# Expert biases in a mixture-of-experts layer: two rows read to one partition each and spread by GpSimd, in place of a 1 MB read to all partitions

## The reference, cut to what matters

```python
gu = lax.ragged_dot(xs, w_gu, group_sizes) + b_gu[sorted_e]     # 1024 -> 2048, the bias is one row of 2048 per expert
gate, up = jnp.split(gu, 2, axis=-1)
gate = jnp.minimum(gate, SWIGLU_LIMIT)
up = jnp.clip(up, -SWIGLU_LIMIT, SWIGLU_LIMIT)
act = (up + 1.0) * (gate * jax.nn.sigmoid(SWIGLU_ALPHA * gate))
out = lax.ragged_dot(act.astype(h.dtype), w_down, group_sizes) + b_down[sorted_e]
out = out * weights.reshape(-1)[order][:, None]
y = jnp.zeros((T, D), dtype=out.dtype).at[tok].add(out)
```

## Time and profile before

| what | value |
|---|---|
| median of the runs | 4029.9 us (4029.44 to 4031.53) |
| the profiled execution's own time | 4033.05 us |
| its span in the profile | 4031.1 us |
| PE busy | 3812.1 us, 95% |
| DVE busy | 2492.9 us, 62% |
| ACT busy | 1613.7 us, 40% |
| POOL busy | 667.9 us, 17% |
| DMA | 813.37 MB, mean 202 GB/s; SP's queue 654.51 MB |
| granted TensorE clock, mean | 0.977 |

### The profile page before, as it was taken

The page is one execution under the profiler, slowest core; times in us unless marked ns, Lnnn a source line. Parts: engine busy times, 40 slices in busy tenths (PEclk is TensorE's granted clock), DMA queues, the critical chain, the costliest instruction groups (busy, mean ns, idle before and its releaser), DMA issues. The chain is left out here.

```text
span 4031.1 us, 66918 instructions
## 1 busy us (share of the span) xinstructions
PE 3812.1 (95%) x17977; PEld 3129.0 (78%) x17978; DVE 2492.9 (62%) x3898; ACT 1613.7 (40%) x2354; POOL 667.9 (17%) x731
## 2 busy tenths in 40 slices
PE   7999999898987999999999999999999999999993
PEld 4887788787876878878877877878888788888782
DVE  5253343596775686576577678577656656656753
ACT  3222321573222464354355455354334434333532
POOL 1110110111221221121111212121121112111202
PEclk9999999899998999999999999999999999999996
DMA  6432441664344797587588787598576667666835
GB/s 236 168 133 84 150 143 69 222 232 150 133 146 154 217 342 221 173 276 225 153 280 286 238 273 257 169 307 266 172 211 208 211 192 230 191 195 180 267 119 190
DMA packets 372676, 813.37 MB, mean 202 GB/s; under 512 B 31449, under 2 KB 31634, under 8 KB 367458
## 3 DMA queue, kind: packets, MB, share of 16 engines
q1 hardware_dynamic: 315826, 654.51, 47.5%
q0 software_dynamic: 53584, 147.48, 14.8%
q10 hardware_dynamic: 3200, 10.53, 0.6%
HBM read 706.18 MB, written 106.23 MB: 202 GB/s over the span
## 5 line engine op out<-in xcount | busy, mean ns | idle before, releaser
L1917 ACT CAST weights_split<-weights_raw 128x1024 fp32r<-128x1024 f32 x468 | 477.7, 1054 | 406.8 <-PE tok_bank_acc L121 284.6
L2012 DVE TENSOR_TENSOR weights_split<-weights_raw,weights_split 128x1024 fp32r<-128x1024 f32 x468 | 545.3, 1217 | 32.4 <-issue 16.4
L2012 DVE TENSOR_TENSOR weights_first<-weights_raw,weights_first 128x1024 fp32r<-128x1024 f32 x464 | 539.1, 1217 | 33.2 <-ACT weights_first L1917 30.3
L1917 ACT CAST weights_first<-weights_raw 128x1024 fp32r<-128x1024 f32 x464 | 471.0, 1050 | 199.3 <-PE tok_bank_acc L121 78.0
L1895 POOL DMA_INDIRECT y_rows<-tok_act_row,tok_token x111 | 200.5, 1806 | 1947.0 <-DVE tok_act_row L2127 1903.6
L119 PE MATMUL tok_bank_acc<-weights_first,weights_split 128*128 128x512 f32 x1136 | 454.3, 400 | 13.4 <-DVE weights_first L2012 10.2
L119 PE MATMUL tok_bank_acc<-weights_split 128*128 128x512 f32 x1136 | 445.4, 392 | 1.2 <-issue 1.1
L121 PE MATMUL tok_bank_acc<-weights_first,weights_split 128*128 128x512 f32 x1136 | 444.1, 391 | 0.0
L120 PE MATMUL tok_bank_acc<-weights_first,weights_split 128*128 128x512 f32 x1136 | 443.1, 390 | 0.0
L121 PE MATMUL tok_bank_acc<-weights_split 128*128 128x512 f32 x1136 | 442.6, 390 | 0.0
L120 PE MATMUL tok_bank_acc<-weights_split 128*128 128x512 f32 x1136 | 442.3, 389 | 0.0
(11 more groups left out here) (377 smaller groups left out, 6838.1 us busy)
## 6 DMA issues: line engine op xcount, KB each, us to landing
weights_raw<-in_w_gu SPq DMA_DIRECT2D x624, 512.0 KB
weights_raw<-in_w_down SPq DMA_DIRECT2D x312, 512.0 KB
tok_bias<-in_b_gu SPq DMA_DIRECT2D x39, 1024.0 KB
early_w_raw<-in_w_in POOLq DMA_DIRECT2D x14, 2048.0 KB, 10.8
proj<-pro_stage SPq DMA_DIRECT2D x112, 256.0 KB, 2.0
pro_w_ada<-in_w_ada POOLq DMA_DIRECT2D x64, 256.0 KB, 3.4
mix_late<-proj SPq DMA_DIRECT2D x48, 256.0 KB, 3.6
mod_w_ada<-in_w_ada SPq DMA_DIRECT2D x8, 1024.0 KB, 15.0
```

Of the source, the lines that this page charges most:

```text
L1917: nc.scalar.copy(whi[c % 2][:, j * SK:(j + 1) * SK], raw[:, n % RAW]).then_inc(hi_done, 1)
L2012: nc.vector.tensor_tensor(wlo[c % 2][:, rows], raw[:, n % RAW], whi[c % 2][:, rows], ALU.subtract).then_inc(lo_done, 1)
```

## The change

The read of 1 MB goes. SP reads the two halves of the next expert's bias row, 1024 floats (4 KB) each, into one partition each, 64 and 96. These lie in the upper half of the tile that now holds both half tile temporaries in its partitions 0 to 63. SP issues them in the middle of a group, after the load of piece 23 and before the loads of the next group's pieces, behind a wait for `bias_set`. POOL spreads each row over the 128 partitions with a `partition_broadcast` into `bias`: for the first group before its loop, and for group g+1 within its turn of group g, after the copies of tokens and shares and before the adds of the down product. It waits there for the group's last activation (which is the last reader of `bias`), for the share copies, the gathered rows and the two bias rows. DVE's first `gate_bias` waits for `bias_set` in place of `bias_in`. The wait for `act_done` on SP goes too.

```diff
-    half_lo, half_gu = k.sb("half_lo", [HR, N]), k.sb("half_gate_up", [HR, N])
+    half_tiles_own = k.sb("half_lo_gate_up", [P, 2, N])
+    half_lo, half_gu = half_tiles_own[0:HR, 0], half_tiles_own[0:HR, 1]
+    bias_rows = [half_tiles_own[p:p + 1].rearrange("p a n -> p (a n)") for p in (HR, HR + 32)]
...
     def sync(sp):
...
         count = field(sp, 0, COUNT, NG)
+        def load_bias_rows(of):
+            for j in range(2):
+                sp.dma_start(bias_rows[j], gu_b[bass.ds(of, 1), j * D:(j + 1) * D]).then_inc(bias_in, 16)
+        load_bias_rows(field(sp, 0, EXPERT, E - 1))
         with sp.Fori(0, NG) as g:
...
-                sp.wait_ge(act_done, G.before * 2 + 1)
-                sp.dma_start(bias[:], gu_b[bass.ds(expert, 1), :].rearrange("o n -> (o n)").partition_broadcast(P)
-                             ).then_inc(bias_in, 16)
                 for n in range(RAW, PIECES * NCH):
                     load(n, expert)
                 next_expert = field(sp, g + 1, EXPERT, E - 1)
                 with sp.If(G.nT > 0):
+                    sp.wait_ge(bias_set, g * 2 + 2)
+                    sp.sem_inc(wait_carrier, 1)
+                    load_bias_rows(next_expert)
                     for n in range(PIECES * NCH, PIECES * NCH + RAW):
                         load(n, next_expert)
...
     def gpsimd(pool):
...
+        def spread_bias(turn):
+            pool.wait_ge(bias_in, turn * 32 + 32)
+            pool.sem_inc(wait_carrier, 1)
+            for j in range(2):
+                nc.gpsimd.partition_broadcast(bias[:, j * D:(j + 1) * D], bias_rows[j], P).then_inc(bias_set, 1)
+                pool.wait_ge(bias_set, turn * 2 + j + 1)
+                pool.sem_inc(wait_carrier, 1)
+        first_full = full_tiles(load_word(pool, 0))
+        pool.wait_ge(rows_in, first_full * 16)
+        pool.sem_inc(wait_carrier, 1)
+        spread_bias(0)
         with pool.Fori(0, NG) as g:
...
                 pool.wait_ge(token_set, g * 2 + 2)
                 pool.sem_inc(wait_carrier, 1)
+                with pool.If(G.nT > 0):
+                    pool.wait_ge(act_done, (G.before + G.U) * 2 + 1)
+                    pool.sem_inc(wait_carrier, 1)
+                    pool.wait_ge(share_set, g * 2 + 2)
+                    pool.sem_inc(wait_carrier, 1)
+                    pool.wait_ge(rows_in, (G.before + G.U + G.nU) * 16)
+                    pool.sem_inc(wait_carrier, 1)
+                    spread_bias(g + 1)
                 for c in (NGU, NGU + 1):
...
         def gate_bias(G, g, q, t):
...
             if q == 0 and t == 0:
-                dve.wait_ge(bias_in, (g + 1) * 16)
+                dve.wait_ge(bias_set, g * 2 + 2)
```

More of the change, by code:

```diff
@@ L1714, in expert_programs @@
      ta_done, ahi_done, alo_done, tx_done, xhi_done, xlo_done, rows_in, y_out0, y_out1, clip_step, wait_carrier,
-     sg_set, word_step, next_set, token_set, share_set, rest_in, pad_set, half_step) = k.sems(
+     sg_set, word_step, next_set, token_set, share_set, rest_in, pad_set, half_step, bias_set) = k.sems(
          "word_set rec_in g2_in g2_set bias_in hi_done lo_done mm_done read_done sg_done act_done "
          "ta_done ahi_done alo_done tx_done xhi_done xlo_done rows_in y_out0 y_out1 clip_step wait_carrier "
-         "sg_set word_step next_set token_set share_set rest_in pad_set half_step")
+         "sg_set word_step next_set token_set share_set rest_in pad_set half_step bias_set")
     rows_left, LEFT = keep["rows_left"], 5
@@ L1728, in weighted_at @@
         if t == HALF:
-            return half_gu[:] if c == NGU + 1 else act_row[0:HR, HALF]
+            return half_gu if c == NGU + 1 else act_row[0:HR, HALF]
         return gu[:, 1] if c == NGU + 1 and t == 0 else act_row[:, t]
@@ L1945, in gate @@
                     act.wait_ge(read_done, G.chunk_tile(2 * q, t))
-                    out, gate_in = (act_row[0:HR, t], half_gu[:]) if t == HALF else (act_row[:, t], gu[:, t % 2])
+                    out, gate_in = (act_row[0:HR, t], half_gu) if t == HALF else (act_row[:, t], gu[:, t % 2])
                     nc.scalar.activation(out, gate_in, ACT.Silu, scale=SIG).then_inc(sg_done, 1)
@@ L2027, in join @@
             if c < NGU:
-                ins = nc.vector.tensor_tensor(half_lo[:], lo, bias[HR:P, column(c):column(c) + N], ALU.add)
+                ins = nc.vector.tensor_tensor(half_lo, lo, bias[HR:P, column(c):column(c) + N], ALU.add)
             else:
-                ins = nc.vector.tensor_copy(half_lo[:], lo)
+                ins = nc.vector.tensor_copy(half_lo, lo)
             ins.then_inc(half_step, 1)
@@ L2043, in gate_bias @@
                 join(G, c)
-                nc.vector.tensor_tensor(half_gu[:], acc[0:HR, bank(c, t)], half_lo[:], ALU.add).then_inc(read_done, 1)
+                nc.vector.tensor_tensor(half_gu, acc[0:HR, bank(c, t)], half_lo, ALU.add).then_inc(read_done, 1)
                 return
             if q == 0 and t == 0:
-                dve.wait_ge(bias_in, (g + 1) * 16)
+                dve.wait_ge(bias_set, g * 2 + 2)
             if q == 0 and t == 1:
@@ L2065, in up_times_gate @@
                 join(G, c)
-                nc.vector.scalar_tensor_tensor(out=half_gu[:], in0=acc[0:HR, bank(c, t)], scalar=1.0, in1=half_lo[:],
+                nc.vector.scalar_tensor_tensor(out=half_gu, in0=acc[0:HR, bank(c, t)], scalar=1.0, in1=half_lo,
                                                op0=ALU.add, op1=ALU.add).then_inc(read_done, 1)
                 dve.wait_ge(read_done, G.chunk_tile(c, t))
-                nc.vector.tensor_scalar(half_gu[:], half_gu[:], LIMIT + 1.0, 1.0 - LIMIT, ALU.min, ALU.max
+                nc.vector.tensor_scalar(half_gu, half_gu, LIMIT + 1.0, 1.0 - LIMIT, ALU.min, ALU.max
                                         ).then_inc(clip_step, 1)
@@ L2072, in up_times_gate @@
                 nc.vector.scalar_tensor_tensor(out=act_row[0:HR, t], in0=act_row[0:HR, t], scalar=float(MOST_GATE),
-                                               in1=half_gu[:], op0=ALU.min, op1=ALU.mult).then_inc(act_done, 1)
+                                               in1=half_gu, op0=ALU.min, op1=ALU.mult).then_inc(act_done, 1)
                 return
@@ L2114, in weigh @@
                         join(G, c)
-                        nc.vector.tensor_tensor(half_lo[:], acc[0:HR, bank(c, t)], half_lo[:], ALU.add).then_inc(half_step, 1)
+                        nc.vector.tensor_tensor(half_lo, acc[0:HR, bank(c, t)], half_lo, ALU.add).then_inc(half_step, 1)
                         dve.wait_ge(half_step, G.halves * 8 + 2 * (c - 1))
-                        nc.vector.scalar_tensor_tensor(out=weighted_at(c, t), in0=half_lo[:], scalar=share[0:HR, t:t + 1],
+                        nc.vector.scalar_tensor_tensor(out=weighted_at(c, t), in0=half_lo, scalar=share[0:HR, t:t + 1],
                                                        in1=g2[0:HR, cols], op0=ALU.mult, op1=ALU.mult).then_inc(read_done, 1)
```

## The result

The change made the kernel slower: 4064.5 us (median of 6 runs, 4060.95 to 4070.55) against 4031.3 us (6 runs on the same chip, 4029.44 to 4032.59), a ratio of 1.0083, interval 1.0073 to 1.0092. The forecast was 4014.5 us, the range up to 4036.

What follows compares the result with a forecast made beforehand. PE was taken to bound the experts' stretch, with DMA short only in ten one-tile groups. Terms -17.4 + 2 = -15.4 us brought the profiled 4033.05 to 4017.6; with the runs' median 3.15 lower, 4014.5 us, range 4004 to 4036.

Steps and rivals of the forecast that it cites:

- What POOL takes from DVE: Spreads on POOL beside DVE's low parts, plus late adds: 0.2 us in each one-tile group, +2 us in all.
- relief: In ten one-tile groups, dropping 39 reads of 1 MB lightens DMA: -17.4 us, bounds 0 and -25.0.
- slower rival: Spreads shut DVE out 5.1 us a group after the last activation; PE loses 3.3 us per one-tile group; 4040 us, chance 0.15.
- long groups: One-tile groups at 1442.9, 2669.8 and 3792.5, DMA always busy: to gain 5.9, 5.6 and 4.5 us, reaching 38 to 40.
- excess: Time of the ten one-tile groups above the shortest, 37.8 us: 25.0 us together, the most a lighter DMA load can give.
- milder ones: The other seven one-tile groups: 7.1 us of excess, of which 5.8 us counted as coming from DMA.
- 21.8 us: Sum of one-tile group gains, 5.9 + 5.6 + 4.5 + 5.8; four fifths taken because DVE is close behind DMA.
- ACT's wait of 5.8 us: In a long one-tile group, ACT's wait for the next weight piece behind the bias read; to be gone if right.
- 9.3 us ahead of the adds: POOL's cover from the last activation to the adds; two spreads of 5.4 to 7.1 us were to fit.
- first group: Spreads lie in POOL's 12.8 us idle time before 1247.0, at worst ending 7.1 us late; nothing counted.
- The rows do arrive late: Where DMA is short, rows come at 2708.9; adds up to 4 to 5 us late, in three groups at most.

Runs made afterwards that it cites:

- e1: Changed kernel with each in-loop spread cut to 8 columns of 1024, so biases are wrong from the second group on: 4024.1 us, 0.9978.
- e7: Changed kernel with POOL also waiting, ahead of the spreads, for the last low part of chunk 5's weights: 4030.6 us, 0.9999.
- e3: Changed kernel with four spreads of 512 columns a group in place of two of 1024: 4064.7 us, 1.0078.
- e4: Changed kernel; DVE makes the second tile's activations low part ahead of chunk 5's last two low parts and the first weighing: 4031.0 us, 1.0001.
- e5: Unchanged kernel (1 MB reads, no spreads) with the same DVE move as e4, as a control: 4017.3 us, 0.9969.
- e2: Unchanged kernel with the 1 MB bias read once ahead of the loop, all groups using the first expert's bias: 4025.1 us, 0.9983.
- e6: Unchanged kernel with e5's edit, and in one-and-a-half-tile groups the half tile's activations low part made early too: 4006.9 us, 0.9942.

## Why the prediction was wrong

**The step that failed** is "What POOL takes from DVE", +2 us, argued from low parts that take 1217 ns "whatever POOL does". What POOL did before could not show it. Its copies took 0.18 us unheld, and its DMA instructions of 0.9 us and more ran beside 202 low parts, of which none took over 1.23 us: a busy POOL alone holds nobody, a broadcast does. Measured, the term is 47 us: 12.6 in the one-tile groups (after less e1), 13.8, 12.6 and 8.0 in those of one and a half, two and three tiles. The 7.8 us of relief taken off, these are the 39.4 us of the stretch but for 0.2; it is a sum of the table's differences, and no second measurement.

The **mechanism** was my slower rival's, and I gave it 0.15. The Trainium skill, SBUF — State Buffer, section "Who interferes with whom", has it that a DVE instruction with two SBUF inputs and a GpSimd instruction that reads SBUF contend, since the second input comes through the read interface that the two share. By that rule this change had to hold DVE up, and the trace agrees: 3.32 us for two low parts instead of 2.35. That whichever starts first keeps the other out for its whole instruction, as I had put it, stands in the section "SBUF: two separate sides" of the same page of the Trainium skill. Here too the trace comes close, once the broadcast's own length is known. It is not the 1.91 us of the middle, but the 1.30 us of a broadcast that waits for nobody, as this one of after, and most of those in e7, which start when the low parts are done:

```profile
1383.95 1.30 POOL L1874 PARTITION_BROADCAST tok_bias<-tok_half_lo_gate_up  x1 [31.80 <-DVE tok_act_row L2102]
```

```profile
L1874 POOL PARTITION_BROADCAST tok_bias<-tok_half_lo_gate_up x78: 1298/1300/5585, 1246.7 to 3834.2; - x78
```

The longer ones have waited for a low part themselves, as the copies did: the one at 1893.32 begins 0.10 us behind a low part, takes 2.29 us, and the next low part is held by it for 0.97 us. Beside the one at 1383.95 a low part that begins 1.02 us behind it takes 1.22 us, that is, isn't held; beside another of 1.30 us, at 1762.37, one that begins 0.89 us behind it takes 1.35 us. So a broadcast of 1.30 us keeps a low part out for its first 1.0 us, and one of 512 columns, 0.80 us unheld in e3, for 0.46. What is left over is 0.3 us both times, about what a broadcast of 8 columns takes (0.27 us in e1).

The **price** was off, then: 2.5 us a spread and 5.1 a group in the rival, 0.97 us and once a group in the runs. The **place** was the other half of the error, and the larger. I looked for slack where DVE's next product is used first, at chunk 5's first low part (slack 1.8 us), and in one-tile groups alone, since those are short of DMA. There the hold decides only from 4.3 us on, and 0.97 us would have cost nothing. But DVE's order is written by hand: every low part that is late moves all that is queued behind it, and what counts is the first in that queue for which PE waits already. In groups of two and three tiles it is the low part of the second tile's activations: PE waited for it 37 times and 11.9 us, 0.36 us in the group shown. In one-tile groups it is the next group's first low part. PE waited 0.70 us for it, and waits 1.54 now; before, this wait was 0.72 us at most behind any of the ten, and now it is 1.5 us or more behind six of them:

```profile
2669.84 0.49 PE L119 MATMUL tok_bank_acc<-weights_first,weights_split 128*128 128x512 f32 x1 [0.70 <-DVE weights_first L2012]
```

```profile
2690.23 0.49 PE L119 MATMUL tok_bank_acc<-weights_first,weights_split 128*128 128x512 f32 x1 [1.54 <-DVE weights_first L2042]
```

Both waits were in the trace of before; I had the total of the second kind and took it for the DMA's. Where such a wait exists there is no slack at all, and the hold is paid in full. e4 and e5 show it for the longer groups: same hold, other order, 33.5 us less, of which the order alone is worth 12.5. For the one-tile groups no run moved what stands behind the hold; there the path is read from the waits alone.

The groups of one and a half tiles lost 2.3 us each, more than the hold. In the one at 2804.5 PE's wait for the half tile is 2.39 us in after, 0.97 more than the 1.42 before:

```profile
2854.14 0.54 PE L2286 MATMUL tok_bank_acc<-weights_first,tok_a_hi 128*128 128x512 f32 x1 [2.39 <-DVE tok_a_hi L2138]
```

```profile
2832.48 0.50 PE L2256 MATMUL tok_bank_acc<-weights_first,tok_a_hi 128*128 128x512 f32 x1 [1.42 <-DVE tok_a_hi L2108]
```

and right behind the longer one comes a spell of 3.4 us at a granted clock of 0.50, the lower level, which the group of before doesn't have:

```profile
2854.50:2857.90 3.40, 3.40 (x10) 2.66 (x9) 0.20 (x1) 1.19 (x2) 1.64 (x1) 0.50 0.80 220
```

Such spells in the experts' stretch went from 4 to 10, and five of the ten lie in the six groups of one and a half tiles; the one of them without a spell took 60.7 us, 1.0 more than before. At half speed 3.4 us do the work of 1.7, so by estimate six more are about 10 of the 47 us. They do not follow from the wait alone: in e4 PE waits for the half tile as long as here (14.3 us in six waits), and one of its six groups has a spell.

**The relief**, -17.4 us, had the right sign and not the size: 7.8 us (e1), 8.3 in e2's groups, 6.9 by its ratio. Most of the miss is in the long groups, for which I took 16.0 us and e2 got 8.0: I had forecast 38 to 40 us, and in e2 they took 40.9, 39.9 and 42.4. Part of their excess was the clock's. I took off one spell at half clock, in the group at 1403.3, but the other three lie in the groups at 1442.9 and 3792.5 (clock 0.96 and 0.92); at 1.7 us each, an estimate, that is 5 of their 12.3 us. In the milder ones, for which I took 5.8 us, 0.2 to 0.3 came. That DVE was close behind DMA there (34 to 36 busy us in 38), for which I took off a fifth, fits this and is not shown to be the reason. 7.8 of the 21.8 us would have been a third left.

**Right:** DMA moved 813.37 MB before and moves 772.80 MB now, 41 MB less. Half right: ACT's wait of 5.8 us, which was to be gone, is 3.65 us at the same place:

```profile
2697.77 2.18 ACT L1947 CAST weights_first<-weights_raw 128x1024 fp32r<-128x1024 f32 x2 [3.65 <-DMA weights_raw<-in_w_gu]
```

A broadcast takes 1.30 us of its own, 1.7 forecast, and up to 1.0 us more where it waits for a low part, as forecast (two of the 78 take longer). Two fit under the 9.3 us ahead of the adds. In the first group, where nothing was counted, the first gate came at 1252.3 us against 1251.1, behind two spreads of which this is the first, and the group took 112.9 us against 112.0:

```profile
1247.78 2.06 POOL L1874 PARTITION_BROADCAST tok_bias<-tok_half_lo_gate_up  x1 [14.87 <-issue]
```

The rows do arrive late where DMA is short, as forecast: POOL waited for them in six groups, 96.4 us in all. A gate waited for the bias once, for 1.5 us: this first one.

**Open.** What starts a spell at the lower clock, and why the last 0.3 us of a broadcast keep nobody out: that the hold covers the part in which the row is read and written is only my guess, though it fits the broadcasts of 512 and of 8 columns. A broadcast placed behind chunk 4's adds, with the adds' own timing kept, was not tried, nor was a second bias tile, which would let the spread lie anywhere in the group.

## What to carry to other kernels

Before work is put on a second engine, look up whether the two engines share a way to memory, and price the hold not by where it falls but by the first consumer behind it, in the order that is written by hand, that has no slack: a wait of 0.36 us repeated in every group says that each further microsecond may be paid in full. If such a wait is there, mend the order first: e6 is worth 23 us by moving two short instructions, more than the transfer that was to go (6 to 8 us). A saturated resource in ten groups of 39 is worth at most the excess of those groups, here 8 of 25 us, so test the removal by itself (e2) before paying for its replacement.

## What the runs showed of the hardware

A partition broadcast of 128x1024 f32 on POOL takes 1.30 us when nothing holds it (e7: 1.30 in the middle), and 1.91 in the middle and 3.27 at most in after, where most of them wait for a low part of DVE; one of 512 columns takes 0.80 us unheld, one of 8 columns 0.27. A DVE instruction with two SBUF inputs that meets one is held 0.97 us at 1024 columns and 0.46 us at 512, that is the broadcast's own length less 0.3 us. Cutting the broadcast up moved the holds without lessening their sum (38 and 38.8 us). POOL's DMA instructions, 0.9 us and more, held none of 202 low parts. And spells of 3.4 us at PE's lower clock came in ten places of the experts' stretch instead of four; in the group at 2804.5 one came right behind a wait that had grown by 1 us, and the group lost 2.6.
